# The first tile's layer norm, one step later in VectorE's order

## The reference

```
h = x @ w_in                       # q 512 | k 128 | v 128 | u 512 | gv 512
A = windowed attention(q, k, v)    # 8 heads, softmax with a learned sink per head
B = gelu(u) * (tril(W_s) @ LN(gelu(gv)) + b)
x = LN1(alpha * x + concat(RMS(A), RMS(B)) @ w_o)
x = LN2(alpha * x + moe(x))        # 16 experts, top 2 of the best group
```

## Time and profile before

| | |
|---|---|
| median of 3 runs | 1161.46 us (1160.75 to 1166.99) |
| profiled execution, its own time | 1164.74 us |
| its span, first to last instruction | 1163.1 us |
| PE busy | 1043.3 us, 90% |
| DVE busy | 894.6 us, 77% |
| ACT busy | 718.1 us, 62% |
| mean granted clock of TensorE | 0.950 |

### The profile page before, as it was taken

How to read it: one execution, slowest core, us unless ns; L and a number is a source line. 1 busy time by engine, 2 the same in 40 slices (tenths; PEclk the granted TensorE clock), 3 DMA queues, 4 the chain that set the end, 5 groups by cost and what they waited for, 6 DMA issues and landing times.

```text
span 1163.1 us, 16849 instructions
## 1 busy us (share of the span) xinstructions
PE 1043.3 (90%) x5403; PEld 875.7 (75%) x5403; DVE 894.6 (77%) x1148; ACT 718.1 (62%) x887; POOL 188.7 (16%) x162
## 2 busy tenths in 40 slices
PE   5999999969989999999389999998799999999950
PEld 4988888857878888887278878887677888888840
DVE  2696674579978999887757858646897888888956
ACT  2424765356868888877524266734576888787852
POOL 3000000016421101110020000000372311221100
PEclk9999889979989999999799999899899999999985
DMA  9423120339999999997734222020799999999934
GB/s 316 160 80 110 40 78 19 110 103 318 366 344 379 387 385 384 385 375 303 222 103 145 81 83 92 27 101 27 248 303 381 376 381 392 379 379 378 374 120 163
DMA packets 117061, 273.27 MB, mean 235 GB/s; under 512 B 10304, under 2 KB 13344, under 8 KB 116992
## 3 DMA queue, kind: packets, MB, share of 16 engines
q1 hardware_dynamic: 101232, 236.80, 56.6%
q0 software_dynamic: 14464, 33.01, 8.1%
q10 hardware_dynamic: 1296, 2.62, 0.6%
HBM read 262.02 MB, written 25.22 MB: 247 GB/s over the span
## 4 chain that ended last, share of the span: by engine, by line
PE 57%; DMA 17%; DVE 10%; issue 6%; ACT 4%; DVEq 3%; POOL 3%; SPq 0%; ACTq 0%; POOLq 0%
DMA raw_far<-in_w_gate 9%; PE bankA L2093 9%; PE bankA L1801 8%; PE bankB L2093 7%; PE bankB L1801 7%; PE bankC L2116 5%; PE bankD L2116 5%; PE bankC L1801 3%; POOL slot_rows L727 3%; PE bankD L1801 3%; PE bankG L1881 3%; DVE w_lo L453 2%; PE bankE L1789 2%; PE bankF L1789 2%; ACT w_hi L447 2%
## 5 line engine op out<-in xcount | busy, mean ns | idle before, releaser
L453 DVE TENSOR_TENSOR w_lo<-raw,w_hi 128x2048 fp32r<-128x2048 f32 (+1 forms) x152 | 340.7, 2261 | 57.1 <-ACT w_hi L447 54.1
L447 ACT ACTIVATE w_hi<-raw 128x2048 fp32r<-128x2048 f32 (+1 forms) x152 | 287.1, 1893 | 120.9 <-PE bankC L1801 40.9
L453 DVE TENSOR_TENSOR w_lo<-raw_far,w_hi 128x2048 fp32r<-128x2048 f32 x64 | 146.4, 2288 | 14.5 <-ACT w_hi L447 14.5
L447 ACT ACTIVATE w_hi<-raw_far 128x2048 fp32r<-128x2048 f32 x64 | 122.8, 1919 | 46.8 <-PE bankB L2093 22.6
L2093 PE MATMUL bankA<-w_hi,xe_hi 128*128 128x512 f32 x256 | 100.7, 394 | 3.4 <-DVE xe_lo L468 3.2
L2093 PE MATMUL bankB<-w_hi,xe_hi 128*128 128x512 f32 x256 | 102.8, 402 | 0.6 <-DVE w_lo L453 0.6
L2093 PE MATMUL bankB<-w_hi,xe_lo 128*128 128x512 f32 x256 | 100.1, 391 | 0.0
L2093 PE MATMUL bankA<-w_hi,xe_lo 128*128 128x512 f32 x256 | 99.9, 390 | 0.0
L2093 PE MATMUL bankB<-w_lo,xe_hi 128*128 128x512 f32 x256 | 99.8, 390 | 0.0
L2093 PE MATMUL bankA<-w_lo,xe_hi 128*128 128x512 f32 x256 | 99.8, 390 | 0.0
L707 POOL DMA_INDIRECT y_rows<-expert_out,idx x32 | 47.9, 1495 | 189.0 <-ACT expert_out L1005 181.3
(11 more groups left out here) (430 smaller groups left out, 2459.5 us busy)
## 6 DMA issues: line engine op xcount, KB each, us to landing
raw<-in_w_up SPq DMA_DIRECT2D x64, 1024.0 KB, 11.3
raw_far<-in_w_gate SPq DMA_DIRECT2D x60, 1024.0 KB, 12.3
raw<-in_w_down SPq DMA_DIRECT2D x60, 1024.0 KB, 12.3
raw<-in_w_in SPq DMA_DIRECT2D x12, 1024.0 KB, 8.8
raw<-in_w_o SPq DMA_DIRECT2D x8, 1024.0 KB, 5.5
x_rows<-x POOLq DMA_DIRECT2D x10, 512.0 KB, 3.0
raw<-in_w_gate SPq DMA_DIRECT2D x4, 1024.0 KB, 8.2
raw_far<-in_w_down SPq DMA_DIRECT2D x4, 1024.0 KB, 12.3
```

What stands on the lines that cost most here:

```text
L447: act.activation(w_hi[:, s % RB, :, 0:n], raw_unit(s)[:, :, 0:n], ACT.Copy).then_inc(hi_done, 1)
L453: dve.tensor_tensor(w_lo[:, s % RB, :, 0:n], raw_unit(s)[:, :, 0:n], w_hi[:, s % RB, :, 0:n].bitcast(F32), ALU.subtract).then_inc(lo_done, 1)
```

## The change

DVE's `layer_norm` is cut in two. The statistics of a tile stay where they were; the rest (`centre`, `spread`) of tile 0 moves to step 4, behind `scores_max(4)`, `rms_norm(2)` and `logits_out(0)` and ahead of `mixed_out(1)`. ACT's `root(0)` moves behind the third and fourth turned pair of tile 2, ahead of `mixed_hi(1)`. For the tiles 1 to 4 nothing is moved.

```diff
@@ ACT, step t @@
                     probs_out(t - 1, range(2))
-                    root(t - 3)
+                    if t > 3:
+                        root(t - 3)
                     probs_out(t - 1, range(2, 4))
+                    if t == 3:
+                        root(0)
                     mixed_hi(t - 2)
@@ DVE @@
+                def statistics(t):
+                    row_stats(t).then_inc(var1_done, 1)
+                    dve.drain()
+
                 def layer_norm(t):
-                    row_stats(t).then_inc(var1_done, 1)
-                    dve.drain()
                     if t == 0:
@@ DVE, step t @@
                     if t >= 4:
                         logits_out(t - 4)
+                    if t == 4:
+                        layer_norm(0)
                     mixed_out(t - 3)
...
                     if t < NT + 1:
-                        layer_norm(t - 3)
+                        statistics(t - 3)
+                        if t > 3:
+                            layer_norm(t - 3)
                         attention_out(t - 1)
                         mixed_lo(t - 2)
```

More of the change, by code:

```diff
@@ L1326, in spread, with layer_norm @@
                     return dve.scalar_tensor_tensor(out=xt, in0=xt, scalar=rs[:, t:t + 1], in1=shift, op0=ALU.mult, op1=ALU.add)
-                def layer_norm(t):
+                def statistics(t):
                     row_stats(t).then_inc(var1_done, 1)
                     dve.drain()
+                def layer_norm(t):
                     if t == 0:
```

## The result

Time before is 1162.60 us, median of 13 runs (1154.43 to 1166.99); time after is 1151.78 us, median of 13 runs. Twelve of these lie between 1147.57 and 1155.29; one slow run of 1221.52, at a mean granted clock of 0.828 where the others had 0.956 to 0.963, stands outside the comparison. The ratio is 0.9904 with an interval of 0.9879 to 0.9929: about 1% faster, as forecast (1151.1 against 1151.78). The forecast of 1151.1 started from the 1161.46 of three runs; the medians of 13 lie 10.8 apart, where 10.4 was forecast. The profiled execution took 1149.51 with a span of 1148.0 and a mean clock of 0.958; PE was busy 1036.6 us (90%), DVE 894.5 (78%), ACT 719.0 (63%).

What follows compares the result with a forecast made beforehand. ACT's root(0), waiting for the variance, held copies PE needed; PE idled, then ran at half clock. Gains of 5.1 and 5.3 us, 10.4 in all, took the median from 1161.46 to 1151.1 us, range 1147.5 to 1157.

Steps and rivals of the forecast that it cites:

- zero: Start of the fourth pair's turn on PE, from which times in a step are counted: 156.92 and 725.96 before.
- the ruler of step 4: Step 4, same instructions without the root's wait, at full clock, supplied step 3's offsets: `mixed_hi` 2.88 us after the turn's start.
- The size: `output(1)` in step 3 would start 5.1 us earlier in layer 0 and 5.3 in layer 1, 10.4 us together.
- the wait alone: PE's shorter idle time ahead of step 3's value sums, without the clock: 2.64 us in layer 0, 2.9 in layer 1.
- the rival of a fall without an idle time: PE's clock falls anyway in step 3's stretch without dense products; gain 5.5 us, time 1155.9, chance 0.10.
- No drain on the table load: On ACT, ahead of the moved root: load priced at 1.28 us without drain, against the skill's 2.66 us switch.
- The norm in step 4: DVE's norm of 2.72 us fits ahead of `mixed_out(1)`'s wait for bank B, with 0.45 us of cover in layer 0.
- the rival "slower": DVE's norm lands on the path and `mixed_out(1)` comes 2.72 us later; time 1162.5, or 1167.4 with clock loss; chance 0.03.
- GpSimd and the loads: GpSimd's constant copies land near 180 beside `layer_norm(1)`, costing nothing; rival: layer 1's expert loads swallow its gain, 1156.4, chance 0.06.
- left in place, the norm could take up to 1.5 us of each gain back: In step 3, an unmoved norm would delay DVE's division and `mixed_lo(1)` to near 161.9, costing up to 1.5 us.
- that cover gone, each late tenth shows as a tenth: The moved root on ACT has 0.13 us of cover before `mixed_hi(1)`; lateness beyond it costs its own length.
- the rival in which the root shows: The moved root holds `mixed_hi(1)` by up to 1.3 us per layer; gain 7.8 us, time 1153.7, chance 0.04.

Runs made afterwards that it cites:

- experiment 2: Kernel before with only tile 0's norm moved to step 4, root(0) left ahead of the last two copies; ratio to the kernel before 1.0014.
- experiment 7: Kernel before plus ten unused 512-column products on PE ahead of the third pair's sums, where PE would stand idle; ratio to the kernel before 0.9939.
- experiment 9: Kernel after with tile 0's norm earlier in step 4, right behind tile 4's maxima and ahead of `rms_norm(2)`; ratio to the kernel before 0.9893.
- Experiment 4: Kernel after with tile 0's norm one place later, behind `mixed_out(1)` and ahead of tile 1's statistics; ratio to the kernel before 0.9978.
- experiment 1: Kernel before with only root(0) moved behind the turned pairs, tile 0's norm left in step 3; ratio to the kernel before 1.0035.
- experiment 6: The repetition: kernel before with only root(0) moved, tile 0's norm left in step 3, run once more; ratio to the kernel before 1.001.
- experiment 10: Kernel after plus a one-column exponential on ACT behind root 0, pulling the next table load ahead of `mixed_hi(1)`; ratio to the kernel before 1.0012.
- experiment 3: Kernel before plus ten 512-column products on PE, placed behind sums that themselves wait for ACT; ratio to the kernel before 1.0024.

## Why the prediction was right, and where a step of it was not

- **ACT's wait for the variance set the step, and DVE's norm stood behind it.** Shown: with the root left in its place the step is what it was (experiment 2), and with both edits `mixed_hi` starts 2.88 and 2.89 after zero, as the ruler of step 4 said, and `output(1)` 5.90 and 5.91 after zero, where 5.91 was forecast.
- **The size.** `output(1)` comes 5.13 and 5.28 us earlier against its zero, 5.1 and 5.3 forecast; between the marks it is 5.15 and 5.30. All later steps moved with it. The sum is right in its terms and not only in total: the wait alone was priced at 2.64 and 2.9 of the gain, the clock at the remainder, and experiment 7 separates them at 2.67 and 2.89 against 2.48 and 2.41 between the marks. That layer 0 agrees to 0.03 is partly luck, since from zero the wait comes out at 2.90. The profiles differ by 15.1 us and the medians by 10.8; only the latter is to be set beside the forecast.
- **The clock holds through transposes and sums.** It stayed at 1.00 from 157.5 to 166.8, of which the part up to 161.3 is transposes and sums alone; the rival of a fall without an idle time did not come true, and experiment 7 speaks against it too. By the Trainium skill (TensorE: Matmul & The Clock Gate, "Part 4: PE-mode transpose") a transpose does not count as work for the clock as a product does; the trace does not bear this out for this mixture.
- **No drain on the table load.** The load took 1.28 us (159.38), the root followed at 160.67. The Trainium skill (ScalarE: Activation LUTs, "What ACT_TABLE_LOAD costs") has 2.66 for the switch; the trace has half of that.
- **The norm in step 4.** Cover forecast 0.45 in layer 0, measured 0.52, and experiment 9 shows that more cover brings nothing. Experiment 4 shows the rival "slower" in a milder form: one place later and 2.0 to 3.5 us per layer are back.
- **GpSimd and the loads.** The copies came later than forecast, 182.25 to 183.74 instead of near 180 (1.2 of it is only where this execution has its zero), since their load took 5.0 us from its issue where it had taken 3.0; so they stood beside `attention_out(3)` and not `layer_norm(1)`. That they cost nothing came out as taken, though beside another instruction. The experts of layer 1 moved with the pipeline.
- **Mis-sized: "left in place, the norm could take up to 1.5 us of each gain back".** It takes 4.0 to 5.3 of the 5.15 and 5.30 (experiment 1 and its repetition). I had followed DVE only to `mixed_lo(1)`. The read of bank A behind it, for which `output(1)` waits, I did not follow, nor that PE, idle for 2.6 us there, lost its clock again, as it did in all four layers of the two executions. The forecast did not rest on it, since the norm moves in this change, but a forecast for the root alone would have been wrong by its whole gain, and my expectation of experiment 1 was.
- **Mis-sized: "that cover gone, each late tenth shows as a tenth".** 1.39 us late gave 7.6 to 7.9 (experiment 10). 1.9 of it had come by the start of `output(1)` (7.81 after zero instead of 5.91); the rest came behind it, at half clock. So the rival in which the root shows, at 1153.7, was priced too low: a root that is late by some 1.3 us would, by experiment 10, have left next to nothing of the gain. For lateness between 0 and 1.39 no run here has a number.

What stays open: experiment 1 was slower in total, 1.0035, though its two steps were each 1.1 us shorter. Its repetition was 1.001, which its interval does not tell from either. The profile can't account for the difference: the profiled execution was the fastest of twelve, 1156.30 against a median of 1166.94. Open is also what decides whether the clock falls behind an idle time of 1.3 or 1.8 us.

## What to carry to other kernels

When you take a wait out of an in-order queue, follow every engine behind it to its next buffer release, not just to the next operation of the chain: here one wait was two, ACT's copies behind the root and DVE's read of a bank behind the norm, and removing either alone brought nothing. Price an idle time of TensorE with the slower stretch that follows it; here it was nearly half of the gain. A neighbouring step of the same loop without the stall, with one event as zero, gave the offsets to within hundredths. And where the cover is small, price what a miss would start, not only the miss.

## What the runs showed of the hardware

- An idle time of PE of 1.3 us was followed by half clock in 7 of 22 layers at one place (cost 3.2 to 3.9 us), while in experiment 10 the same 1.3 us, at another place, was followed by it in both layers, for 13.7 us each, through products without a gap. An idle time of 1.8 us was followed by it in one of two layers (experiment 4), one of 2.5 to 2.7 us in all ten (the kernel before, experiments 1, 2, 3 and 6).
- A table load took 1.28 us and the next instruction followed within 0.02 us, also where two loads stood 1.61 us apart (157.97 and 159.58 in experiment 10).
- The stage of the experts takes 281.3 to 288.2 us from execution to execution of kernels that are the same there. Two profiles can thus differ by more than this change is worth, and a step is to be compared between marks close around it.
- Ten products whose results nobody reads, put into PE's idle time, made the kernel before 0.6% faster (experiment 7, 0.3 to 0.9%); behind the wait they brought nothing (experiment 3).
